# End of the S5 stage: the gated unit's first weight tile split by GpSimd, VectorE's last two passes together, that tile's products between the state products

## What is computed

```python
u = h @ w_in                                   # 512 x 1024
lam_bar = exp(lam * dt); b_bar = ((lam_bar - 1) / lam) * b
hs = scan(h_t = lam_bar * h_{t-1} + b_bar u_t) # complex, 64 groups x 64 states
y = real(c @ hs) + d * u
g = gelu(y)
ab = g @ w_glu + b_glu                         # 1024 x 2048, the gated unit
val, gate = split(ab)
out = val * sigmoid(gate)
```

## Time and profile before

| | |
|---|---|
| median of 3 runs | 2184.24 us |
| the profiled execution | 2186.4 us, of this 2184.7 us span |
| TensorE busy | 2100.3 us (96%), 9784 matmuls |
| VectorE, ScalarE, GpSimd busy | 1213.5 (56%), 692.8 (32%), 229.9 us (11%) |
| TensorE's granted clock, whole run | 0.988 of full |
| head of the S5 stage, its eight projections, end of its last pass | 840 to 857, 857 to 950, 950 to 984 us |
| the gated unit up to its last product | to 1063 us |

### The profile page before, as it was taken

One profiled execution on the slowest core, in us unless ns is written; L12 is line 12 of the kernel. 1 busy time (PEld: TensorE's weight loads), 2 busy tenths in 40 slices (PEclk: granted clock), 3 DMA queues, 4 the chain that ended last, 5 costly groups with the idle time before them and its releaser, 6 DMA issues.

```text
span 2184.7 us, 24655 instructions
## 1 busy us (share of the span) xinstructions
PE 2100.3 (96%) x9784; PEld 1412.2 (65%) x9784; DVE 1213.5 (56%) x1726; ACT 692.8 (32%) x1040; POOL 229.9 (11%) x257
## 2 busy tenths in 40 slices
PE   7999898998999989999999999999999999999997
PEld 3544444333333335778788888878877788888886
DVE  2875833344443336987665565576885636343434
ACT  3223422110111105223332232256893424232231
POOL 0010000003300018920000000000110000000000
PEclk9999999999999999989999999999999999999999
DMA  9844355999999992226354544313432222222221
GB/s 384 313 167 155 103 236 206 426 427 424 427 426 427 426 421 99 81 72 241 135 183 167 170 166 171 128 58 128 156 124 78 96 97 78 97 96 96 97 96 57
DMA packets 113703, 433.26 MB, mean 198 GB/s; under 512 B 7854, under 2 KB 13106, under 8 KB 100936
## 3 DMA queue, kind: packets, MB, share of 16 engines
q1 hardware_dynamic: 93896, 360.02, 43.0%
q0 software_dynamic: 19712, 71.93, 9.1%
HBM read 429.13 MB, written 6.36 MB: 199 GB/s over the span
## 4 chain that ended last, share of the span: by engine, by line
PE 64%; PEld 15%; DVE 7%; issue 6%; DMA 5%; ACT 2%; DVEq 1%; POOLq 0%; SPq 0%; PEldq 0%; POOL 0%; ACTq 0%
PE PS L1223 8%; PE PS L794 6%; PE PS L798 6%; PE PS L797 6%; PEld PS L794 5%; PEld PS L798 5%; PEld PS L797 4%; PE PS L1246 4%; PE PS L926 4%; DMA work<-in_w_dn 3%; PE PS L1508 3%; PE PS L1512 3%; PE PS L1511 3%; PE PS L1363 3%; PE PS L1260 2%
## 5 line engine op out<-in xcount | busy, mean ns | idle before, releaser
L798 PE MATMUL PS<-work_f32r,work_f32r 128*128 128x512 f32 x1168 | 454.9, 389 | 0.0
L794 PE MATMUL PS<-work_f32r,work_f32r 128*128 128x512 f32 x768 | 300.6, 391 | 1.7 <-DVE work_f32r L3058 1.0
L797 PE MATMUL PS<-work_f32r,ring_f32r 128*128 128x512 f32 x768 | 299.3, 390 | 0.0
L2258 DVE TENSOR_TENSOR ring_f32r<-ring,work_f32r 128x2048 fp32r<-128x2048 f32 x100 | 227.8, 2287 | 121.5 <-ACT work_f32r L1662 121.1
L1662 ACT ACTIVATE work_f32r<-ring 128x2048 fp32r<-128x2048 f32 x100 | 190.2, 1910 | 297.1 <-DMA ring<-in_mlp_w 245.6
L798 PEld LDWEIGHTS PS<-work_f32r,work_f32r 128*128 128x128 f32 x1168 | 219.5, 188 | 45.8
L1223 PE MATMUL PS<-work 128*64 128x512 f32 x752 | 170.6, 597 | 2.7 <-ACT work L1863 2.2
L794 PEld LDWEIGHTS PS<-work_f32r,work_f32r 128*128 128x128 f32 x768 | 144.7, 188 | 32.7 <-DVE work_f32r L3058 1.5
L797 PEld LDWEIGHTS PS<-work_f32r,ring_f32r 128*128 128x128 f32 x768 | 144.7, 188 | 30.2 <-issue 0.2
L794 PE MATMUL PS<-h_f32r,work_f32r 128*128 128x512 f32 x400 | 155.9, 390 | 1.4 <-DVE work_f32r L2278 1.4
L797 PE MATMUL PS<-h_f32r,ring_f32r 128*128 128x512 f32 x400 | 155.6, 389 | 0.0
(11 more groups left out here) (454 smaller groups left out, 3372.4 us busy)
## 6 DMA issues: line engine op xcount, KB each, us to landing
work<-in_w_gu SPq DMA_DIRECT2D x47, 2048.0 KB, 20.2
ring<-in_mlp_w SPq DMA_DIRECT2D x64, 1024.0 KB, 5.2
work<-in_w_dn SPq DMA_DIRECT2D x24, 2048.0 KB, 24.3
ring<-in_w_gu SPq DMA_DIRECT2D x16, 2048.0 KB, 25.2
work<-in_ada_w_2T POOLq DMA_DIRECT2D x16, 1536.0 KB, 6.9
ring<-in_m_w_in SPq DMA_DIRECT2D x20, 1024.0 KB, 5.2
work<-in_w_adaT POOLq DMA_DIRECT2D x8, 2048.0 KB, 11.3
work<-in_ada_w_2T POOLq DMA_DIRECT2D x32, 512.0 KB, 3.6
```

Of the source, the lines that this page charges most:

```text
L794: mm = nc.tensor.matmul(PS[:, bank + k, :], f32r(w_of), f32r(hi(c)), start=first and c == 0, stop=False)
L797: nc.tensor.matmul(PS[:, bank + k, :], f32r(wlo), f32r(hi(c)), start=False, stop=False)
L798: mm = nc.tensor.matmul(PS[:, bank + k, :], f32r(w_of), f32r(lo(c)), start=False, stop=last and c == 3)
L2258: tt(f32r(ring[:, s, at, :]), ring[:, s, at, :], f32r(tiles[s][:, at, :]), ALU.subtract).then_inc(w_split, 1)
```

## The change

Seven edits. (1) GpSimd, behind its last doubling, subtracts both halves of the first weight tile (128x2048 each); VectorE's two splits of it go. (2) VectorE goes from pass 6 with only one remainder between to pass 7; the scalings of x for 6 and 7 and the remainders 5 to 7 come behind. (3) TensorE: column 0 of the first half goes ahead of the states of pass 6, columns 1 to 3 ahead of those of pass 7, and the second half is done by chunks of rows (`glu_second(c)`, 12 matmuls each, on all four columns), the first between the turnings of 6 and 7. Banks of the turnings and their waits follow. (4) ScalarE rounds both halves one after the other behind k = 6, and the second tile's first half ahead of its last rounding. (5) The hi tiles are laid out by halves, so that both halves of the first tile lie on angle tables of passes 0 to 3. (6) GpSimd's two copies of the powers of C become four multiplications by one (`ones`, broadcast), 128x1024 each, and move ahead of the clearing of `k_mat`, with their wait for the experts' end. (7) VectorE waits for `K_ZERO` before its lag copies.

```diff
@@ -264,7 +264,7 @@
         hi_tiles = [ring_hi[:, 0, :, :], ring_hi[:, 1, :, :]]
-        glu_tiles = [wk(20480, KC, TN), wk(4096, KC, TN)]
+        glu_tiles = [[wk(20480, 4, TN), wk(4096, 4, TN)], [wk(22528, 4, TN), wk(6144, 4, TN)]]
         g_both = wk(12288, KC, 2 * T)
@@ -297,12 +297,15 @@
 
+        def hi_half(tiles, s, half):
+            return glu_tiles[s][half] if tiles is glu_tiles else tiles[s][:, 4 * half:4 * half + 4, :]
+
         def tok_bank(n):
...
         def turned_bank(q):
-            return 4 if q == KC - 1 else 7
+            return 4 if q == KC - 2 else 7
 
@@ -357,7 +360,7 @@
         s5_angles_set, s5_set, x2_begun, experts_done = (sem(n) for n in ("s5_angles_set", "s5_set", "x2_begun", "experts_done"))
-        C_SET, B_SET, K_ZERO, C_COPIED, RIMS_ZERO = range(1, 6)
+        C_SET, B_SET, C_COPIED, K_ZERO, RIMS_ZERO = range(1, 6)
 
@@ -695,12 +698,15 @@
                 nc.gpsimd.tensor_tensor(x2_sq[:, c, :], x[:, c, :], x[:, c, :], ALU.mult).then_inc(sq_added_x2, 1)
+            pool.wait_ge(experts_done, 1)
+            one = ones[:, 0:1].broadcast_to([P, 2 * S5_TILES * HP])
+            for j in range(1, S5_J + 1):
+                power = (c_early[:, j, :, :] if j < S5_J else c_last).rearrange("p a h -> p (a h)")
+                nc.gpsimd.tensor_tensor(c_pow[:, j, :, :].rearrange("p a h -> p (a h)"), power, one, ALU.mult)
+            pool.drain()
+            pool.sem_inc(s5_set, 1)
             pool.wait_ge(padded, 2)
             pool.memset(k_mat, 0.0).then_inc(s5_set, 1)
-            pool.wait_ge(experts_done, 1)
-            nc.gpsimd.tensor_copy(c_pow[:, 1:S5_J, :, :], c_early[:, 1:S5_J, :, :])
-            pool_step(nc.gpsimd.tensor_copy, c_pow[:, S5_J, :, :], c_last)
-            pool.sem_inc(s5_set, 1)
             pool.memset(decay_now[:, :, 0:1], 0.0)
@@ -724,6 +730,11 @@
                 pool.sem_inc(s5_set, 1)
+            for half in range(2):
+                pool.wait_ge(w_hi, SPLITS["glu"] + half + 1)
+                at = slice(4 * half, 4 * half + 4)
+                nc.gpsimd.tensor_tensor(f32r(ring[:, 0, at, :]), ring[:, 0, at, :], f32r(glu_tiles[0][half]), ALU.subtract) \
+                    .then_inc(w_split, 1)
 
@@ -790,7 +801,7 @@
                         at = slice(k * P, (k + 1) * P)
-                        w_of, wlo = tiles[s][:, 4 * half + c, at], ring[:, s, 4 * half + c, at]
+                        w_of, wlo = hi_half(tiles, s, half)[:, c, at], ring[:, s, 4 * half + c, at]
                         mm = nc.tensor.matmul(PS[:, bank + k, :], f32r(w_of), f32r(hi(c)), start=first and c == 0, stop=False)
@@ -1404,7 +1415,9 @@
                 pe.wait_ge(gelu_done, q + 1)
-                if 0 < q < KC - 1:
+                if q == KC - 1:
+                    pe.wait_ge(lo_ready, KC - 2)
+                elif 0 < q < KC - 2:
                     pe.wait_ge(lo_ready, q)
@@ -1438,19 +1451,30 @@
 
+            def glu_second(c):
+                pe.wait_ge(lo_ready, LOWS["glu"][0] + c + 1)
+                pe.wait_ge(w_split, SPLITS["glu"] + 2)
+                for k in range(4):
+                    at = slice(k * P, (k + 1) * P)
+                    w_of, wlo = hi_half(glu_tiles, 0, 1)[:, c - 4, at], ring[:, 0, c, at]
+                    nc.tensor.matmul(PS[:, k, :], f32r(w_of), f32r(glu_hi[:, c, :]), start=False, stop=False)
+                    nc.tensor.matmul(PS[:, k, :], f32r(wlo), f32r(glu_hi[:, c, :]), start=False, stop=False)
+                    mm = nc.tensor.matmul(PS[:, k, :], f32r(w_of), f32r(glu_lo[:, c, :]), start=False, stop=(c == KC - 1))
+                    if c == KC - 1:
+                        mm.then_inc(glu_mm, 1)
+
             inputs_to_states(KC - 1)
             within_chunks(KC - 1)
+            glu_first((0,))
             states_to_outputs(KC - 2)
             outputs_turned(KC - 3)
-            glu_first((0, 1))
+            glu_first((1, 2, 3))
             states_to_outputs(KC - 1)
             outputs_turned(KC - 2)
-            glu_first((2,))
+            glu_second(4)
             outputs_turned(KC - 1)
-            glu_first((3,))
-            pe.wait_ge(lo_ready, LOWS["glu"][0] + KC)
-            split_half(SPLITS["glu"], 0, 1, 0, lambda c: glu_hi[:, 4 + c, :], lambda c: glu_lo[:, 4 + c, :], False, True,
-                       None, glu_mm, glu_tiles, False)
+            for c in range(5, KC):
+                glu_second(c)
 
@@ -1698,7 +1722,7 @@
                 at = slice(4 * half, 4 * half + 4)
-                copy(f32r(tiles[s][:, at, :]), ring[:, s, at, :]).then_inc(w_hi, 1)
+                copy(f32r(hi_half(tiles, s, half)), ring[:, s, at, :]).then_inc(w_hi, 1)
 
@@ -1983,11 +2007,11 @@
                 if k == KC - 2:
-                    round_half(first, 0, 0, glu_tiles)
-                elif k == KC:
+                    round_weights(first, 0, glu_tiles)
+                elif k == KC + 1:
                     act.wait_ge(state_ready, KC)
-                    round_half(first, 0, 1, glu_tiles)
-            round_weights(first, 1, glu_tiles)
+                    round_half(first, 1, 0, glu_tiles)
+            round_half(first, 1, 1, glu_tiles)
             for i in range(2):
@@ -2255,7 +2279,7 @@
                 at = slice(4 * half, 4 * half + 4)
-                tt(f32r(ring[:, s, at, :]), ring[:, s, at, :], f32r(tiles[s][:, at, :]), ALU.subtract).then_inc(w_split, 1)
+                tt(f32r(ring[:, s, at, :]), ring[:, s, at, :], f32r(hi_half(tiles, s, half)), ALU.subtract).then_inc(w_split, 1)
 
@@ -2749,6 +2773,7 @@
             lags = PS[:, 7, :].rearrange("p (q n) -> p q n", q=KC)
+            dve.wait_ge(s5_set, K_ZERO)
             for a in range(2, 4):
@@ -2798,14 +2823,22 @@
             dve.wait_ge(s5_set, RIMS_ZERO)
+            def outputs_scaled(q):
+                stt(x[:, q, :], x[:, q, :], col("g_final", q), first_rstd, ALU.mult, ALU.mult).then_inc(xn_ready, 1)
+
             for q in range(KC):
                 dve.wait_ge(s5_set, quads_turned(q))
-                if q == KC - 1:
-                    split_weight_half("glu", 0, 0, 0, glu_tiles)
                 s5_quad(q)
-                stt(x[:, q, :], x[:, q, :], col("g_final", q), first_rstd, ALU.mult, ALU.mult).then_inc(xn_ready, 1)
-                if q >= 2:
+                if q < KC - 2:
+                    outputs_scaled(q)
+                if 2 <= q < KC - 1:
                     outputs_rest(q - 2)
+            outputs_rest(KC - 3)
+            outputs_scaled(KC - 2)
+            outputs_rest(KC - 2)
+            outputs_rest(KC - 1)
+            outputs_scaled(KC - 1)
+
             def mod_pair(j):
@@ -2814,9 +2847,6 @@
 
-            split_weight_half("glu", 0, 0, 1, glu_tiles)
-            outputs_rest(KC - 2)
-            outputs_rest(KC - 1)
             split_weights("glu", 2, 1, glu_tiles)
```

## The result

Over 12 runs the changed kernel took 2188.6 us in the median (2185.24 to 2192.46), the kernel before 2184.29 beside it. The ratio is 1.0019, 95% interval 1.0012 to 1.0027: 2.6 to 5.9 us slower, about the 0.2% that the prediction called the limit of no change. Its profiled execution spans 2188.2 us against 2184.7. So the kernel became slightly slower, inside the predicted range (2178.5 to 2190.8), 2.0 us above the predicted time; the forecast of +2.4 us lies just under the interval.

What follows compares the result with a forecast made beforehand. TensorE fills most of the span, so the change matters only where it waits or runs at the lower clock; +6.4 us at the head and -4.0 at the end give +2.4, 2186.6 us, range 2178.5 to 2190.8.

Steps and rivals of the forecast that it cites:

- Parts 1 and 2: End of S5: VectorE's shorter path to pass 7 and TensorE's new order end the first tile 10.8 us earlier, VectorE undisturbed.
- Part 3: End of S5: GpSimd's split and VectorE exclude each other, new 3.5 us wait at pass 5, gain cut to 4.0 us.
- I let pass 5 begin 0.6 us earlier than now: End of S5: VectorE's pass 5 assumed to start 0.6 us earlier because GpSimd's turning ends earlier against the rest.
- Part 4: Head: GpSimd's four multiplications of 1.93 us hold VectorE's doublings, so TensorE goes on 3.7 us later.
- Part 5: Head: TensorE's longer idle time drops the clock for 6 us, costing 2.7 us more; head 6.4 us in all.
- rival (d): Head: the clock stays low through the first projection, +5.5 us, 2189.7 us; chance 0.15.
- Sum: Whole kernel: +6.4 us at the head and -4.0 at the end make +2.4, giving 2186.6 us.
- (b): Head and end: long GpSimd arithmetic lets VectorE through, -1.1 and -10.8 us, 2172.3 us; chance 0.14.
- (c): One of the two places is spared: head spared 2179.1 us, end spared 2179.8 us; chance 0.14.
- (e): End: VectorE's last remainders come too late, TensorE waits as now, the head's loss stays, 2190.6 us; chance 0.05.

Runs made afterwards that it cites:

- end_cleared: end_alone with GpSimd clearing the two weight halves (reading nothing) instead of splitting them: 2174.84 us, ratio to the kernel before 0.9945.
- end_vector: end_alone with the split back on VectorE, first half before pass 6, second behind pass 7: 2176.40 us, ratio to the kernel before 0.9955.
- end_alone: The changed kernel with the head of the kernel before (powers of C copied in the old place): 2184.49 us, ratio to the kernel before 0.9990.
- head_alone: The kernel before with only the head edit (powers of C as four multiplications before the clearing, VectorE's wait for K_ZERO): 2190.39 us, ratio 1.0026.
- after_warm: The changed kernel with more filler products (28 instead of 6 in the timeline) while TensorE waits at the head: 2184.98 us, ratio to the kernel before 0.9997.
- end_vector_late: end_vector with GpSimd's two old copies of the powers of C held until VectorE's doublings are through: 2177.51 us, ratio to the kernel before 0.9959.
- end_pieces: end_alone with each half of GpSimd's split cut into four instructions of 512 elements: 2181.71 us, ratio to the kernel before 0.9979.
- end_held_later: end_alone with GpSimd's split held back until the states of pass 5 are set: 2182.52 us, ratio to the kernel before 0.9991.

## Why the prediction was right, and where not

**Parts 1 and 2, the ends of VectorE and TensorE: right.** 10.8 us were forecast for an undisturbed VectorE; 10.2 (end_cleared) and 9.8 (end_vector) were measured. Passes 6 and 7 have no wait in the change. What ScalarE's two roundings together cost wasn't measured apart; it would be part of the missing 0.6 to 1.0. One reading of the sum was wrong without harm: at 846.00 four, not six, operations of 256 elements were left in the doublings.

**Part 3, the exclusion: right in mechanism, short in size.** Both held rows are there (4 to 6 us forecast, 5.32 and 5.52 measured), and so is the one new wait before pass 5. Alone, the end gave 3.61 us for 4.0 forecast, with a wait of 3.83 for 3.5; the clock's share there, 10.8 - 3.83 - 0.3 - 3.61, is 3.1 for 3.0. In the change it gave 1.69: the wait was 4.79, and by the same sum the clock took 4.0. (With end_cleared's 10.2 both clock figures are 0.6 less.) The step that failed is "I let pass 5 begin 0.6 us earlier than now". Pass 5 began 1.1 us later against the projection. Therefore VectorE was still in its scan (948.62 to 950.96) when the rounding released GpSimd at 950.05, the first half came before both rotations, and the second half ended with one rotation (1.15 us) still to come besides the states, where I had the states alone. end_alone, with pass 5 at its old 82.02, goes as I had written it. The reason I gave (GpSimd's turning ends earlier) was true, at 79.3 instead of 82.8 us behind the projection, but the turning began 1.6 us earlier against the projection and delayed VectorE more on its way: from the start of pass 3 to that of pass 4 VectorE took 13.7 us instead of 12.9. That it does so by meeting other two-input operations there is my reading; that the head's edit causes it is shown: head_alone has the same 83.10 with none of the end's edits, end_alone the old 82.02, and after_warm goes back. An earlier turning isn't a later pass in general: in end_vector_late the turning began later, and so did pass 5, and at the one value -6.13 pass 5 stood anywhere from 81.60 to 82.12. So the head part made the end part worse, in the traces by 1.9 us: 1.0 is the longer wait, the rest the clock, which was low for 10.2 us instead of 6.8 and, as below, isn't bound to the edit. By the ratios the parts add up, 0.26% - 0.10% = 0.16% against 0.19% measured, each known to about 0.09%, so over many executions this extra loss isn't shown. I had the turning 2.7 us earlier against the rest where it was 1.6, and drew from it an earlier pass 5 where a later one came.

The Trainium skill's page SBUF — State Buffer, section Who interferes with whom, says that two SBUF inputs on VectorE exclude a GpSimd instruction that reads SBUF, and not one that only writes. These runs agree with both halves of it: 5.3 us beside a reading instruction of 2048 elements, 1.23 beside the clearing. The Trainium skill's page GPSIMD Engine Reference, section Elementwise — side-by-side cycle accounting, has 4497 ns for such an instruction of 2048 elements. That fits too: 10.67 us for two halves with one VectorE operation of 1.2 between leave at most 4.7 each.

**Part 4, the head: right in mechanism, 1.0 too large.** Four VectorE operations of about 1.9 us were forecast; four came (the first is the copy at 841.25). The doublings ended at 853.85, not at 854.5, because GpSimd was through at 848.13, not at 848.7: I gave each multiplication 1.93 us where it took 1.87, and left short gaps between them where there were none. Later start of the statistics' products: 2.9 by the timeline (counted from the last scatter product 2.7), not 3.7.

**Part 5, the clock at the head: right that it falls, 1.1 too large.** It stood at 0.50 for some 3.4 us (855.8 to 859.2), not 6, and cost 1.63 (after_warm), not 2.7. So it was full again before the projection, and rival (d) did not happen.

**Sum.** Head +4.3 for +6.4, end -1.7 for -4.0: two errors of 2 us of opposite sign, and the sum, +2.7, was near the forecast +2.4 partly by luck. The whole change, by the ratio, is +4.1. Unforeseen were 0.6 us more in the norm behind the gated unit. Before and after, TensorE waits there 2.07 and 2.06 us for the same operation, but only in the change does the clock fall behind it, shown by the filler products that follow:

```profile
1068.80 1.60 PE L782 MATMUL PS<-ones 128*128 128x128 f32 x12
```

```profile
1072.04 2.63 PE L793 MATMUL PS<-ones 128*128 128x128 f32 x12
```

Of the rivals, (b) fell with the held rows, (c) too since both places were held, (e) with the waits of passes 6 and 7 gone. What stays open: why the same wait brings the clock down in one trace and not in another. This wait is 2.05 to 2.08 us long in every trace, and the same fillers behind it take 2.50 to 2.93 us in five of the twelve (the change, end_vector, end_cleared, end_pieces, end_held_later) and 1.60 in the other seven. So it isn't the change that decides it. It is worth 0.6 us here and 0.8 at the end of head_alone, and no run isolates it.

## What to carry to other kernels

Work moved to GpSimd was free for VectorE here only where it didn't read SBUF beside VectorE's two-input instructions; otherwise each such VectorE instruction paid up to one whole GpSimd instruction, so price the move by counting those pairs, and look first for a gap in which VectorE waits for someone else (the 1.61 us before pass 6) and could do the work itself. Reorder first and move second: here the order alone was worth 10 us and the move to GpSimd gave 6 of them back. Two edits in one stage need not be independent when a free-running engine sits between them: write down when each engine's train starts against the others' before adding the parts.

## What the runs showed of the hardware

- The exclusion went instruction by instruction in turn, in all sizes run here, up to 2048 elements: beyond its own time VectorE lost 1.1 us beside pieces of 512 elements, some 0.8 beside a copy of 1024, 1.7 beside a multiplication of 1024, 4.1 to 4.3 beside a subtraction of 2048, and nothing beside a clearing of 2048. A scaling with a per-partition factor and two SBUF tensors is held too (5.04 us), and so is a plain copy from SBUF to SBUF (1.36 us for 32 elements at 841.25, 0.19 in the kernel before).
- A GpSimd copy of 1024 elements took 1.02 us, a multiplication by one of the same elements 1.87.
- TensorE's clock stood at 0.50 for 3.4 us at the head of the change, 6.8 in end_alone (960.1 to 966.9) and 10.2 at the end of the change, with idle times of 3.75, 3.83 and 4.79 us. The idle time doesn't set it: with 2.34 us it was 6.8 in the kernel before (961.4 to 968.2), with 2.51 us 3.4 in end_pieces (968.6 to 972.0), and with 2.06 us it fell in five traces of twelve. I had taken one figure, 6 us, for all.
